# Taking the last three k steps of each row-wise product token tile by token tile

## The reference, cut to what matters

```python
x = x + _rmsnorm(merged @ w_o[i], g_post_mix[i])
...
x = x + _rmsnorm((jax.nn.gelu(a) * v) @ w_down[i], g_post_ffn[i])
...
gate = jax.nn.sigmoid((x @ w_ple_gate[i]).astype(jnp.float32)).astype(x.dtype)
x = x + _rmsnorm(e * gate, g_ple[i])
...
h = h + rms_norm(mix, a_norm_post[a])      # mix = o @ w_out
...
ff = squared_relu_mlp(rms_norm(h, mlp_norm_pre[layer]), mlp_w_up[layer], mlp_w_down[layer])
h = h + rms_norm(ff, mlp_norm_post[layer])
```

## Time and profile before

| what | value |
| --- | --- |
| median of 3 runs | 2498.8 us (2498.57, 2498.8, 2508.07) |
| span of the profiled execution | 2496.0 us |
| its own time | not recorded apart from its span |
| TensorE busy | 2278.2 us (91%) |
| VectorE busy | 1074.6 us (43%) |
| ScalarE busy | 802.2 us (32%) |
| GpSimd busy | 231.2 us (9%) |
| matmuls of the row-wise products (L1747) in the chain that ended last | 17% of the span |

### The profile page before, as it was taken

How to read it: one execution, slowest core, us unless ns; L and a number is a source line. 1 busy time by engine, 2 the same in 40 slices (tenths; PEclk the granted TensorE clock), 3 DMA queues, 4 the chain that set the end, 5 groups by cost and what they waited for, 6 DMA issues and landing times. The chain is left out here.

```text
span 2496.0 us, 27307 instructions
## 1 busy us (share of the span) xinstructions
PE 2278.2 (91%) x10845; PEld 1843.3 (74%) x10845; DVE 1074.6 (43%) x1905; ACT 802.2 (32%) x1469; POOL 231.2 (9%) x339
## 2 busy tenths in 40 slices
PE   6967998998999999799987889999989888899998
PEld 5846655467888787589977678878779657788787
DVE  5311454346555434423488253333443473433333
ACT  3221354224333323332201242232342463322322
POOL 8100000001000000200254010000110010100000
PEclk9988799999999999899867889999999789899999
DMA  5374001132333222132200123322233101222222
GB/s 134 97 95 91 22 1 34 34 101 79 99 101 101 85 101 86 59 101 85 68 1 1 51 76 101 102 85 101 85 127 119 51 1 51 93 86 100 101 87 82
DMA packets 168252, 192.02 MB, mean 77 GB/s; under 512 B 22866, under 2 KB 146045, under 8 KB 168125
## 3 DMA queue, kind: packets, MB, share of 16 engines
q1 hardware_dynamic: 163680, 176.15, 22.3%
q0 software_dynamic: 3904, 13.97, 3.1%
q10 hardware_dynamic: 541, 0.15, 0.0%
HBM read 182.91 MB, written 7.34 MB: 76 GB/s over the span
## 5 line engine op out<-in xcount | busy, mean ns | idle before, releaser
L1136 DVE TENSOR_TENSOR WHL<-raw,WHL 128x1024 fp32r<-128x1024 f32 x312 | 386.3, 1239 | 743.9 <-ACT WHL L748 743.8
L748 ACT ACTIVATE WHL<-raw 128x1024 fp32r<-128x1024 f32 x312 | 328.5, 1053 | 655.1 <-PE bank L1747 414.4
L1663 PE MATMUL bank<-HXh,WHL 128*128 128x512 f32 x1248 | 492.6, 395 | 42.1 <-DVE WHL L1136 38.3
L1747 PE MATMUL bank<-WHL,HXh 128*128 128x512 f32 x1888 | 512.5, 394 | 18.6 <-DVE HXl L1144 12.3
L1665 PE MATMUL bank<-HXh,WHL 128*128 128x512 f32 x1248 | 488.1, 391 | 0.0
L1747 PEld LDWEIGHTS bank<-WHL,HXh 128*128 128x128 f32 x1888 | 358.8, 190 | 96.4 <-issue 19.2
L1664 PE MATMUL bank<-HXl,WHL 128*128 128x512 f32 x1056 | 413.0, 391 | 0.0
L1663 PEld LDWEIGHTS bank<-HXh,WHL 128*128 128x128 f32 x1248 | 236.5, 189 | 92.4 <-DVE WHL L1136 38.8
L1747 PE MATMUL bank<-WHL,HXl 128*128 128x512 f32 x880 | 273.2, 392 | 0.0
L1665 PEld LDWEIGHTS bank<-HXh,WHL 128*128 128x128 f32 x1248 | 236.0, 189 | 49.7
L1664 PEld LDWEIGHTS bank<-HXl,WHL 128*128 128x128 f32 x1056 | 200.0, 189 | 40.4
(11 more groups left out here) (259 smaller groups left out, 2598.1 us busy)
## 6 DMA issues: line engine op xcount, KB each, us to landing
raw<-in_mlp_w_up_dram SPq DMA_DIRECT2D x64, 512.0 KB, 4.5
raw<-in_mlp_w_down_dram SPq DMA_DIRECT2D x64, 512.0 KB, 4.4
raw<-in_w_up_dram SPq DMA_DIRECT2D x44, 512.0 KB, 5.0
raw<-in_a_w_in_dram SPq DMA_DIRECT2D x32, 512.0 KB, 4.5
raw<-in_w_in_dram SPq DMA_DIRECT2D x24, 512.0 KB, 4.8
raw<-in_w_down_dram SPq DMA_DIRECT2D x22, 512.0 KB, 4.2
raw<-in_w_kv_dram SPq DMA_DIRECT2D x16, 512.0 KB, 4.5
rel_dram<-PB POOLq DMA_DIRECT2D x1, 5120.0 KB, 54.8
```

The lines of the kernel that those rows point to most:

```text
L748: return a.activation(dst, src, ACT.Copy, **k)
L1136: v.tensor_tensor(dst(1), src, dst(0).bitcast(F32), ALU.subtract).then_inc(w_lo, 1)
L1663: m.matmul(b[:, :], w[0][:, k, :], x[0][:, k, :], start=(k == 0), stop=False)
L1747: ins = m.matmul(bank[2 * tt + h][:, :], x, w[:, h * HALF:(h + 1) * HALF], start=(k == 0 and i == 0), stop=(k == nk - 1 and i == 2))
```

## The change

The steps up to nk-4 run k by k; the last three run tile by tile, in the order nk-3, nk-2, nk-1 for each tile. Unit nk-3 is given free after its group for tile 3, as nk-2 is. Nothing but the order of TensorE's instructions and the places of their waits and signals is different.

```diff
-                for k in range(nk - 2):
+                for k in range(nk - 3):
                     w = unit(name, k)
                     x_ready_for(k)
                     for tt in range(TT):
                         ins = products(k, tt, *w)
                     ins.then_inc(ring_used, 1)
 
-                x_ready_for(nk - 2)
-                w0 = unit(name, nk - 2)
+                tail = []
                 for tt in range(TT):
-                    ins = products(nk - 2, tt, *w0)
-                    if tt == TT - 1:
-                        ins.then_inc(ring_used, 1)
-                    if tt == 0:
-                        x_ready_for(nk - 1)
-                        w1 = unit(name, nk - 1)
-                    products(nk - 1, tt, *w1).then_inc(s_last, 1)
+                    for k in range(nk - 3, nk):
+                        if tt == 0:
+                            x_ready_for(k)
+                            tail.append(unit(name, k))
+                        ins = products(k, tt, *tail[k - nk + 3])
+                        if k == nk - 1:
+                            ins.then_inc(s_last, 1)
+                        elif tt == TT - 1:
+                            ins.then_inc(ring_used, 1)
```

## The result

| | before | changed |
| --- | --- | --- |
| median | 2498.69 us (4 runs) | 2539.55 us (4 runs, 2537.01 to 2542.73) |
| span of the profiled execution | 2496.0 us | 2537.2 us |
| its own time | not recorded apart | 2538.93 us |
| mean granted clock, of 1 | 0.931 | 0.922 |

The ratio is 1.016, with a 95% interval from 1.0144 to 1.0177. The kernel is slower by about 41 us. The forecast was 2532.2 us with a range of 2520 to 2543.

The account below looks back on a forecast made before the run. VectorE's in-order queue was taken to set the gap after each row-wise product. Terms of 25.2 + 6.2 + 1.0 + 0 + 1.0 = 33.4 us on 2498.8 gave 2532.2 us, range 2520 to 2543.

Parts of the forecast that it names:

- The direction and the mechanism: Row-wise tails: unit nk-3 comes free six groups later, ScalarE's split waits, finished tiles wait behind it; slower by 33.4 us.
- One common tail: Gap after `w_o`, `h_out`, `down0`, `d_out`: 6.3 us longer each (5.5 to 6.9), 25.2 us for the four.
- `down`: Gap after this product: late split delays VectorE's multiplications, so the transposes start 6.2 us later (5.6 to 6.7).
- `ple_gate`: Late split, then table load and sigmoids on ScalarE: TensorE gets tile 0's pair 1.0 us late, other tiles on time.
- `down1`: No next weight follows, so nothing blocks, and no backlog is left to remove: 0 us.
- The holes: TensorE's waits for weight unit nk-1 inside seven tails: 0.15 us each, 1.0 us in all (0 to 2).
- Rival 2: TensorE also starves in every tail because unit nk-1 comes late: holes of 1.2 us, 8.4 in all, 2539 us; 5 in 100.
- The clock: Granted clock after the tails: costed at nothing, since TensorE still resumes at 1.2 GHz; 4 us either way over six tails.
- Rival 1: Early tile signals remove VectorE's backlog: 2.0 us less in four tails, 8 in all, 2491 us; 4 in 100.
- Rival 3: GpSimd's roots hold VectorE's additions for 0.57 us: five tails grow by 2.3 each, 11 us, 2543 us; 3 in 100.
- Rival 4: Queues catch up unseen, so the block costs 3 us less in each of five long tails: 2517 us; 7 in 100.
- The signs: Profile after: ScalarE's split waits about 10 us; first transposes wait near 10.5 us in four tails, 8 in `down`.

Follow-up runs that it names:

- experiment 2: Kernel before, old order of matmuls, but unit nk-3 given free only in the last tile's group of step nk-2: 2538.61 us, ratio 1.0152.
- experiment 4: Changed kernel with the split of the next weight's unit 0 moved behind the residual on both engines: 2498.69 us, ratio 0.9991.
- experiment 5: Kernel before with the split of the next weight's unit 0 moved behind the residual: 2500.23 us, ratio 1.0001.

## Why the prediction was right, point by point

- **The direction and the mechanism** were right: the unit comes free at the tenth group, ScalarE's split waits there, and the tiles wait behind it. ScalarE's split waited until 1455.68, 2.5 us before TensorE's last product ended, as forecast. Experiments 2, 4 and 5 show this apart from everything else.
- **One common tail**, 6.3 us: measured 6.2 in each of four, 24.8 for 25.2. The first multiplication was to come 6.9 us later and came 6.94. The waits of 0.38 and 0.23 went, as said. That of 0.77 was to stay and shrank to 0.46, since GpSimd's slow operation is now another, L545, and longer. That is 0.31 us that I had not booked. Against it, of the two waits that went (0.38 and 0.23) only 0.34 and 0.12 were gained: VectorE still pauses 0.10 us between a multiplication and the addition that follows (1457.92 + 1.28 to 1459.30). 6.94 - 0.46 - 0.31 is the 6.2.
- **`down`**, 6.2: measured 6.4. I took a tile at 2.56 us and left out that pause of 0.10 between the multiplication and the addition; in the rows of `h_out` the next multiplication of a full queue comes 2.59 us after the last one (the second at 1460.51, which stands among the rows left out), and three tiles make 0.1 of the difference.
- **`ple_gate`**, 1.0: measured 1.2, of which TensorE's wait for the first sigmoids is 0.98 (the sum behind the forecast, 1004.26 - 1003.35, gives 0.9 and was rounded up); the gate's product starts 1.14 us after the last product, where it started at once before. **`down1`**, 0: measured 0.
- **The holes**, 0.15 each and 1.0 in all: 0.09 in six products, 0.03 in `ple_gate`, 0.6 in all. Rival 2, holes of 1.2 us, is excluded.
- **The clock**, 0 with 4 us either way, is the term that was mis-sized. The terms above give 33.0 where I had 33.4, and the span grew by 41.2. The 8 us between lie where nothing was changed. I had looked for an effect of the clock only next to the tails, within 3 us of work, and not in the long stretches of attention behind them. The 8 us are twice the bound that I had given the term. The time is inside the range all the same, because the upper bounds of the other terms (4.2 us over the sum) and the spread of the medians (3 us) left room for it. That is luck, and not because I had foreseen this.
- **Rival 1** has its condition confirmed by experiment 4: without the split in front, the early signals do take VectorE's backlog away. Its price was too high, 1.5 and not 2.0 us a tail, and even the 6.5 us of shorter gaps did not show in two medians (0.9991 and 1.0013).
- **Rival 3** is excluded: no addition took over 1.29 us in the changed kernel, nor over 1.31 in any of the fourteen profiles. The Trainium skill (SBUF — State Buffer, "Who interferes with whom") says of a VectorE instruction with two SBUF inputs and a GpSimd instruction that reads SBUF that the order of issue decides which one waits. In this case it was always GpSimd's that grew: from 0.22 to 1.31 us (L543, started 0.05 us behind the addition) and from 0.57 to 1.44 (L545, started 0.28 behind it). Where GpSimd was first, by 0.1 us in the earlier trace rows, the addition still took 1.29. So the side of the rule on which VectorE would wait does not show here, although GpSimd was first by up to 0.23 us beside other additions too, and those took 1.29 at most.
- **Rival 4**, 3 us less in each long tail, is excluded: the five are within 0.2 us of their forecasts.
- **The signs** came as told but for two loose ones. ScalarE's split waited 12.6 us behind the split before it, where I had written about 10, and `down`'s transposes 8.71, where my own 6.2 on 2.35 would have given 8.55 and I had written 8. No sign of being wrong showed.

## What to carry to other kernels

When a change moves the place where a ring slot is given free, look up who waits for that slot and what is queued behind the waiting instruction. In an in-order queue one wait for a slot holds up work that is ready and urgent, even if the slot's content isn't needed for long: here TensorE used the new unit first at 1476.04 in `h_out`'s norm, 20 us after the split. A release 8.2 us later cost 6.2 us in each of four products (6.4, 1.2 and 0 in the others), while the new order of the matmuls without that wait left the time within 0.13% of before (0.9991 and 1.0013). Finishing tiles sooner is worth something only for the consumer that can get to them, and the same is true in reverse: without a backlog in front, the next engine in the chain (here GpSimd's roots) takes part of the gain.

## What the runs showed of the hardware that I had not expected

- In a stretch of 260 us that no edit touched, the same 1185 matmuls kept TensorE busy for 229.5 us in one kernel and 236.0 in another, at a mean granted clock of 0.89 and 0.86, and so again in a second profile of each (230.4 and 236.0). A kernel's time can so move by 4 us far from the edit.
- Two profiles of the same kernel, 2496.0 and 2500.1 us, agree to 0.1 us in every gap behind a row-wise product. Of their difference 3.8 us lie in two long stretches, 2.4 ahead of `h_out` and 1.4 ahead of `d_out`.
- GpSimd's operation on 128 numbers took up to 1.44 us instead of 0.57 beside a VectorE addition of two SBUF operands, which itself kept its 1.28 to 1.31.
- A gain of 6.5 us in the gaps did not reach the time: the granted clock fell to 1.2 GHz for 3.4 us about 1 us into each of two products of 174 us, and a stretch between them took 3.3 us more.
